# A 2-layer hybrid decoder step: the sample state products as stacked fp32r products, and the feed-forward norm factor applied behind the products

## The chip, the cores and the metric

The program runs on one core of a Trainium2 chip. The metric is the device time of one launch in microseconds; before and after are each timed in several runs, and the median is compared. Engine names are those of the profile: PE (TensorE matmul), PEld (its weight loads), DVE (VectorE), ACT (ScalarE), POOL (GpSimd), SP (SyncE, which here only issues transfers).

## The reference

Two layers; each layer maps 256 prompt tokens and 32 sample tokens (8 sequences of 4) of width 1024, together T = 288 columns. A layer is feed-forward (FFN) 1, token mixing, FFN 2:

```
def rmsnorm(x, g):
    y = xf * rsqrt(mean(xf * xf) + eps);  return y * g
def swiglu(x, w13, w2):
    a, b = split(x @ w13);  return (silu(a) * b) @ w2
x = x + 0.5 * swiglu(rmsnorm(x, f1n), f1w13, f1w2)
x = x + token_mixing(rmsnorm(x, mn), ...)
x = x + 0.5 * swiglu(rmsnorm(x, f2n), f2w13, f2w2)
```

Part of token mixing is the SSD scan, a recurrence over 32 heads in 8 groups. For the sample tokens it updates a state per sequence and head, h = exp(sum dt*A) h + sum over tokens of (dt x decay) B^T. It is all fp32.

## The kernel before

Activations lie feature-major: a tile of 128 features by 288 columns. An fp32 weight product is made of three fp32r products, weights high half by activations high half, high by low, low by high (`product`, lines 1425 to 1427); the weight halves are made on the chip. Weights come in units of 128 x 2048 in two slots s = 0, 1. For each unit SP loads `raw[s]`, ACT copies it to `w_hi[s]` (`high_unit`, line 676, after PE is done with the slot's previous unit), then DVE (`low_unit`, line 931) or POOL (line 1346) subtracts to `w_lo[s]`, and PE runs 48 matmuls of 288 columns on it. In the FFNs the low halves are DVE's; in the mixing stage they are mostly POOL's. Semaphores order everything; each engine runs its own list in order.

FFN: `norm` on PE sums squares of x (8 tiles, fp32 products with `ones`, line 1510) after ACT has squared them (line 683); ACT takes the root (687), DVE the reciprocal (962) and eight multiplications x * gain * rinv (966), ACT copies to `u_hi` (693), DVE subtracts to `u_lo` (958). Only then does the first weight product start. All of this waits for `add_to_x` (993), which adds the last stage's products to x. `swiglu` then runs 11 pairs of units of w13 (per pair: gate unit in banks 0, 1, up unit in banks 2, 3; silu on ACT, line 701, from PSUM; product and split on DVE, 981, 941, 943), and then the units of w2.

At the top of each layer SP loads ten small tables (`vec_a`, `vec_b`, `rows3`: taps, biases and gains) ahead of the first weights, and PE turns them behind the norm's sums.

SSD: per group g of 8, PE turns tiles of x and B to token-major (1526), DVE scales them (`a_tri` 1215, `xdt` 1230, `xdte` 1240, `xdte_s` 1243), builds `b_diag` (1250), a block-diagonal [32, 8 x 128] matrix with B of each sequence, ACT takes exponentials. After the prompt's products comes, for each of the two tiles t of the group: turn the old state (`state_turn`), two fp32 products `b_diag` by `xdte_s` of 512 columns each (line 1843), then products with the turned state (1850), a copy by ACT (`tok_rows`, 882) and `rows_turn`; DVE updates the state (1279), and the group's last DVE operation, line 1292, lets PE start the next group. Between these, PE runs three half units `side(3g..3g+2)` of unrelated weight products as filler, whose evacuations (846, 849) and weight copies (676) share ACT with the SSD, and whose low halves POOL makes. At the stage's start ACT copies `conv_out` (831) and POOL sends it out by DMA (1391, 1393).

Of the kernel before, what the change touches and what calls it, by code (L numbers as in the profile page):

```python
# [23 lines left out]
P = 128  # L24
# [83 lines left out]

def side_unit(n):

    return (True, n // 3) if n % 3 == 1 else (False, n - (n + 1) // 3)


def constants():
# [10 lines left out]
    small = np.zeros((TS, 2 * TS + NB), f)  # L125
    small[:, :TS] = same & (j[:, None] <= j[None])
    small[:, TS:TS + NB] = j[:, None] // NT == np.arange(NB)[None]
    small[:, TS + NB:] = same & (j[:, None] > j[None])
# [55 lines left out]
def trunk(nc, x_prompt, x_sample, cache_kv_w128, cache_kv_w512, cache_kv_w2048, state_conv, state_ssm,  # L184
# [9 lines left out]

    SKEWED = P * (W_LINE + 1)
# [5 lines left out]
    def place(name, shape, dt=F32, at=None):  # L201
# [3 lines left out]
        if at is None:  # L205
# [23 lines left out]
    small = place("small", [TS, 2 * TS + NB])  # L229
    ident, ones, tri, sgt = (square[:, n, :] for n in range(4))  # L230
    tri_sel_s, sel_s, tri_s, sgt_s = (small[:, 0:TS + NB], small[:, TS:TS + NB], small[:, 0:TS],
                                      small[:, TS + NB:])
# [11 lines left out]
    dt_fm = place("dt_fm", [HEADS, T])  # L244
# [52 lines left out]
    hidden = r("hidden", [P, 2, T])  # L297
    y_out = place("y_out", [P, 2, D], at=F_AT)
# [31 lines left out]
    xdt_s = r("xdt_s", [TS, 256])  # L330
    xdte_s = r("xdte_s", [TS, 256])
    b_tm_s = r("b_tm_s", [TS, NS])
    b_diag = r("b_diag", [TS, NB, NS])
# [7 lines left out]
    y_sq = place("y_sq", [P, KI, T], at=R2 + 4 * 1440)  # L341
# [3 lines left out]
    assert print_free > 24000  # L345
# [3 lines left out]
    with ExitStack() as ctx:  # L349
# [9 lines left out]
        x_first = sem("x_first", 0)  # L359
# [15 lines left out]
        vec_in = sem("vec_in", 16 * 10)  # L375
        vec_turned = sem("vec_turned", 1, 1)
        vec_ready = sem("vec_ready", 1)
        rows_used = sem("rows_used", 1, 1)

        squared = sem("squared", 3 * 4)  # L380
        sum_ready = sem("sum_ready", 3)
        rms_ready = sem("rms_ready", 3)
        normed_part = sem("normed_part", 3 * 4)
# [51 lines left out]

        ssd_turned = sem("ssd_turned", G)
# [60 lines left out]
        def _(sp):  # L497
# [25 lines left out]
            sp.dma_start(small[:], c_small).then_inc(const_in.sem, 16)  # L523

            with sp.Fori(0, DEPTH) as l:

                sp.wait_ge(vec_turned.sem, l + 1)
                settle(sp)
                sp.dma_start(vec_a[:], conv_w[bass.ds(l, 1)].rearrange("a i (t c) -> (a i t) c", c=P))\
                    .then_inc(vec_in.sem, 16)  # L530
                for row, v in ((V_CONVB, conv_b), (V_F1, ffn1_norm), (V_MIX, mix_norm), (V_F2, ffn2_norm),
                               (V_SSD, ssd_norm)):
                    n = v.shape[1] // P
                    sp.dma_start(vec_b[row:row + n, :], v[bass.ds(l, 1)].rearrange("a (t c) -> (a t) c", c=P))\
                        .then_inc(vec_in.sem, 16)
                sp.dma_start(vec_b[V_FIN:V_FIN + KD, :], final_norm.rearrange("(t c) -> t c", c=P))\
                    .then_inc(vec_in.sem, 16)
                sp.wait_ge(rows_used.sem, l + 1)
                settle(sp)
                for n, v in enumerate((dt_bias, a_log, d_skip)):  # L540
                    sp.dma_start(rows3[:, n, :], v[bass.ds(l, 1)].broadcast_to((P, HEADS)))\
                        .then_inc(vec_in.sem, 16)
# [106 lines left out]
                with sp.Fori(0, PAIRS_WO) as i:  # L649
                    rows(m + (M_WO + i), w_o, l, i * 512)  # L650
                with sp.Fori(0, PAIRS_W13) as i:
                    panel(m + (M_W13B + i), ffn2_w13, l, i * 256, FF + i * 256)
# [14 lines left out]
        def _(act):  # L667
# [9 lines left out]

            def norm(l, n, ready, m):
# [11 lines left out]
                for part in range(4):  # L690
                    tiles = slice(2 * part, 2 * part + 2)
                    wait(act, normed_part, l, 4 * n - 3 + part)
                    act.activation(u_hi[:, tiles], full[:, tiles], ACT.Copy).then_inc(u_hi_ready.sem, 1)

            def swiglu(l, m0, e0, n0):
                def body(i):
                    high_unit(0, l * PAIRS + (m0 + 1 + i))

                    act.wait_ge(unit_done[0].sem, l * PAIRS + (m0 + 2 + i))
                    act.wait_ge(evac[1].sem, l * EVACS + (e0 + 1 + i))  # L700
                    act.activation(silu_a[:], ps[:, 0:2, 0:T], ACT.Silu).then_inc(evac[0].sem, 1)
                    high_unit(1, l * PAIRS + (m0 + 1 + i))
                with act.Fori(0, PAIRS_W13) as i:
                    body(i)
# [12 lines left out]
            with act.Fori(0, DEPTH) as l:  # L717
                m = l * PAIRS

                act.wait_ge(x_first.sem, 4)  # L720
                norm(l, 1, R_W2B - ROWS, m)
                swiglu(l, M_W13A, E_W13A, 0)
# [5 lines left out]
                act.activation(dt_fm[:], ps[0:HEADS, 0, 0:T], ACT.Copy).then_inc(evac[0].sem, 1)  # L728
# [43 lines left out]
                act.activation(to_end[0:TS, 3, :], ps[0:TS, 4, 224:256], ACT.Exp).then_inc(to_end_ready.sem, 1)  # L772
# [80 lines left out]
                wait(act, kv_out, l, 16 * 6)  # L853
                for g in range(G):
                    wait(act, ssd_turned, l, g + 1)
                    for c in range(2):
                        act.activation(b_tm[:, c, :], ps[:, 7, c * P:(c + 1) * P], ACT.Copy)
                    act.activation(b_tm_s[:], ps[0:TS, 7, 256:384], ACT.Copy).then_inc(b_ready.sem, 1)
# [53 lines left out]
                norm(l, 3, R_WO, m + M_W13B)  # L912
                swiglu(l, M_W13B, E_W13B, PAIRS_W13)
# [13 lines left out]
        def _(dve):  # L927
# [24 lines left out]

            def norm(l, n, gain):
# [20 lines left out]
            def swiglu(l, m0, e0, n0):  # L974
                with dve.Fori(0, PAIRS_W13) as i:
                    low(l * PAIRS + (m0 + 1 + i))
                    dve.drain()

                    dve.wait_ge(evac[0].sem, l * EVACS + (e0 + 2 + i))
                    dve.wait_ge(unit_done[1].sem, l * PAIRS + (m0 + 2 + i))  # L980
# [967 lines left out]
```

## Time and profile before

| | us |
|---|---|
| median of 3 runs | 2414.03 (2411.07 to 2414.3) |
| profiled execution, its own time | 2411.02 |
| span in the profile, first to last instruction | 2408.9 |
| PE busy, share of the span | 90% |
| DVE, ACT, POOL busy | 53%, 41%, 17% |

The span and the profiled execution's own time differ by 2.1 us, which lies around the instructions. A busy PE is not PE at its peak: a row's duration of a matmul is its latency, and the spacing of many matmuls is read from a window and a count.

### The profile page before, as it was taken

To read this page: it belongs to the slowest core of one execution; us is meant where nothing else is said; L and a number is where in the kernel's file an instruction comes from. 1 tells how busy PE (TensorE), PEld (TensorE's weight loads), DVE (VectorE), ACT (ScalarE), POOL (GpSimd) and SP (SyncE) were. 2 spreads that over 40 slices of the span, in tenths; PEclk is the share of its full clock that TensorE was granted. 3 is DMA by queue.
4 is the path that set the end of the run, shared out by engine and by line. 5 is a ranking of instruction groups with operands and counts; after the bars stand their busy time and mean duration, and the time that the engine had idled before them with its cause. 6 is when DMAs were issued, how large, how long until landed. Compare 5 with 4: busy or idle time off the path is not lost.

```text
span 2408.9 us, 38626 instructions
## 1 busy us (share of the span) xinstructions
PE 2166.7 (90%) x15100; PEld 2000.4 (83%) x15100; DVE 1283.7 (53%) x1936; ACT 996.8 (41%) x1153; POOL 414.4 (17%) x162
## 2 busy tenths in 40 slices
PE   7999899987889888899899989999798888969996
PEld 5999889975767688899889989899676667969996
DVE  3553455765666472554355443575666665444543
ACT  3552434344344432554355443343433434235532
POOL 2000002202332455000000000121122224630000
PEclk9999999888999999999999999897998899989998
DMA  6444544423333333354434436442333332434541
GB/s 205 162 160 149 172 145 135 136 71 106 114 115 118 99 123 123 122 167 164 142 124 161 156 128 196 143 131 88 92 93 112 118 116 92 156 105 141 172 157 55
DMA packets 258232, 317.06 MB, mean 132 GB/s; under 512 B 9070, under 2 KB 232846, under 8 KB 258010
## 3 DMA queue, kind: packets, MB, share of 16 engines
q1 hardware_dynamic: 249656, 287.92, 37.0%
q0 software_dynamic: 7776, 26.73, 3.7%
q8 instruction: 77, 1.26, 0.2%
q10 hardware_dynamic: 680, 0.80, 0.1%
q14 instruction: 43, 0.35, 0.0%
HBM read 291.44 MB, written 26.33 MB: 132 GB/s over the span
## 4 chain that ended last, share of the span: by engine, by line
PE 69%; DVE 11%; ACT 5%; PEld 5%; issue 4%; POOL 3%; DVEq 1%; DMA 1%; SPq 1%; PEldq 0%; ACTq 0%; POOLq 0%
PE ps L1425 18%; PE ps L1427 17%; PE ps L1426 17%; PE ps L1526 5%; ACT w_hi L676 3%; POOL w_lo L1346 3%; PE ps L1843 2%; DVE flat L1292 2%; DVE w_lo L931 2%; PEld ps L1701 1%; PE ps L1510 1%; PEld ps L1425 1%; PE ps L1791 1%; PEld ps L1426 1%; PEld ps L1427 1%
## 5 line engine op out<-in xcount | busy, mean ns | idle before, releaser
L1425 PE MATMUL ps<-u_hi,w_hi 128*128 128x288 f32 x2736 | 851.8, 311 | 51.3 <-DVE u_lo L958 39.8
L1426 PE MATMUL ps<-u_lo,w_hi 128*128 128x288 f32 x2736 | 833.0, 304 | 0.0
L1427 PE MATMUL ps<-u_hi,w_lo 128*128 128x288 f32 x2736 | 830.2, 303 | 0.0
L676 ACT ACTIVATE w_hi<-w_raw 128x2048 fp32r<-128x2048 f32 x249 | 476.3, 1913 | 657.1 <-PE ps L1427 628.8
L931 DVE TENSOR_TENSOR w_lo<-w_raw,w_hi 128x2048 fp32r<-128x2048 f32 x172 | 394.3, 2292 | 549.1 <-ACT w_hi L676 549.1
L1425 PEld LDWEIGHTS ps<-u_hi,w_hi 128*128 128x128 f32 x2736 | 539.1, 197 | 62.0 <-issue 56.9
L1426 PEld LDWEIGHTS ps<-u_lo,w_hi 128*128 128x128 f32 x2736 | 540.4, 198 | 0.7
L1427 PEld LDWEIGHTS ps<-u_hi,w_lo 128*128 128x128 f32 x2736 | 539.9, 197 | 0.0
L1346 POOL TENSOR_TENSOR w_lo<-w_raw,w_hi 128x2048 fp32r<-128x2048 f32 x77 | 355.6, 4618 | 612.9 <-ACT w_hi L676 612.7
L1425 PE MATMUL ps<-h_hi,w_hi 128*128 (+1 forms) x704 | 209.2, 297 | 14.6 <-DVE w_lo L931 14.6
L1427 PE MATMUL ps<-h_hi,w_lo 128*128 (+1 forms) x704 | 207.9, 295 | 0.0
L1426 PE MATMUL ps<-h_lo,w_hi 128*128 (+1 forms) x704 | 207.8, 295 | 0.0
L1383 POOL DMA_DIRECT2D out_dram<-kv_p x6 | 4.1, 678 | 852.3 <-DVE kv_s L1093 852.1
L1425 PEld LDWEIGHTS ps<-h_hi,w_hi 128*128 128x128 f32 x704 | 132.8, 189 | 17.4 <-DVE w_lo L931 11.5
L1426 PEld LDWEIGHTS ps<-h_lo,w_hi 128*128 128x128 f32 x704 | 132.9, 189 | 0.0
L1427 PEld LDWEIGHTS ps<-h_hi,w_lo 128*128 128x128 f32 x704 | 132.7, 188 | 0.0
L1114 DVE SCALAR_TENSOR_TENSOR acc<-flat,conv_wt,acc 128x312 f32<-128x312 f32 x192 | 104.5, 586 | 7.3
L1279 DVE SCALAR_TENSOR_TENSOR h<-h,e_s,ps 128x128 f32<-128x128 f32 x256 | 68.9, 341 | 54.7 <-PE ps L1843 54.7
L1425 PE MATMUL ps<-y_hi,w_hi 128*128 128x288 f32 (+1 forms) x256 | 78.8, 308 | 9.4 <-POOL w_lo L1346 9.4
L676 ACT ACT_TABLE_LOAD x45 | 57.7, 1283 | 69.5 <-DMA w_raw<-in_ffn_w_dram 69.4
L1427 PE MATMUL ps<-y_hi,w_lo 128*128 128x288 f32 (+1 forms) x256 | 77.2, 302 | 0.0
L1426 PE MATMUL ps<-y_lo,w_hi 128*128 128x288 f32 (+1 forms) x256 | 77.2, 301 | 0.0
(273 smaller groups left out, 2706.4 us busy)
## 6 DMA issues: line engine op xcount, KB each, us to landing
w_raw<-in_ffn_w_dram SPq DMA_DIRECT2D x128, 1024.0 KB, 5.0
w_raw<-in_w_in_dram SPq DMA_DIRECT2D x82, 1024.0 KB, 5.3
h<-in_state_ssm_dram SPq DMA_DIRECT2D x32, 512.0 KB, 4.1
out_dram<-h POOLq DMA_DIRECT2D x32, 512.0 KB, 3.9
w_raw<-in_w_ssd_out_dram SPq DMA_DIRECT2D x16, 1024.0 KB, 4.8
kv_in<-in_cache_kv_w_dram SPq DMA_DIRECT2D x32, 256.0 KB, 4.2
w_raw<-in_w_o_dram SPq DMA_DIRECT2D x8, 1024.0 KB, 4.8
w_raw<-in_ffn_w_dram SPq DMA_DIRECT2D x8, 512.0 KB, 3.3
```

The costliest lines, as they stand in the source:

```text
L676: act.activation(w_hi[s][:], raw[s][:], ACT.Copy).then_inc(hi_ready[s].sem, 1)
L931: dve.tensor_tensor(w_lo[s][:], raw[s][:], w_hi[s][:].bitcast(F32), ALU.subtract)\
L1114: last = dve.scalar_tensor_tensor(out=dst, in0=src, scalar=tap, in1=dst, op0=ALU.mult, op1=ALU.add)
L1279: dve.scalar_tensor_tensor(out=h0[tile % 3][:, b, :], in0=h0[tile % 3][:, b, :], scalar=e_s[:, t, TS + b:TS + b + 1], in1=ps[:, 6 + b // 4 ...
L1292: last = dve.scalar_tensor_tensor(out=flat[:, tile, TP:T], in0=flat[:, tile, TP:T], scalar=skip[:, tile:tile + 1], in1=off_s[:, t, :], op0 ...
L1346: pool.tensor_tensor(w_lo[s][:], raw[s][:], w_hi[s][:].bitcast(F32), ALU.subtract)\
L1425: pe.matmul(out, wh, hi, start=first, stop=False)
L1426: pe.matmul(out, wh, lo, start=False, stop=False)
L1427: return pe.matmul(out, wl, hi, start=False, stop=last)
L1510: last = pe.matmul(ps[:, 0, 0:T], ones, full[:, k, :], start=(k == 0), stop=(k == KD - 1))
L1526: return pe.transpose(out, src, square[0:p, 0, 0:p])
L1843: last = pe.matmul(ps[:, 6 + n, :], xdte_s[:, t * P:(t + 1) * P], b_diag[:, 4 * n:4 * n + 4, :].rearrange("p b n -> p (b n)"), start=True, ...
```

## The change

1. FFN norm (FFN 1 and FFN 2 of both layers; the mixing norm stays as it was). `u = x * gain` is split at once, without the factor rinv: ACT writes `u_hi` with eight scaled copies, DVE writes `u_lo` with eight scalar_tensor_tensor, and PE starts `first_unit`, which goes over k outside and the two banks inside. The squares of x are taken by ACT in one activation behind that, DVE adds the eight tiles in three operations, PE sums over partitions with one fp32 product after the first pair of units. DVE's `gate` multiplies the gate product by rinv from PSUM to `a_in`, ACT's silu reads `a_in` from SBUF, and DVE's `up` multiplies silu by rinv and then by the up product. The first pair of units uses banks 0 to 3, the second 4 to 7, and the loop follows from the third. In the loop DVE makes the low half of slot 1 behind `up` instead of before it. The low half of slot 1 of FFN 2's first pair goes from POOL to DVE.
2. The small tables are gathered by 13 POOL transfers at the very start into `vec_tables` in DRAM; the first layer's are loaded by SP before the loop, each next layer's by two transfers ahead of FFN 2's weights, and PE turns them in FFN 2. SP keeps three small loads at the top of the layer.
3. SSD, sample part: `xdte_s` and `b_tm_s` are made on 96 partitions, three copies of the 32 tokens (POOL's `stack_sample` copies the columns three times, and a transpose puts them on partitions). `x_stack` holds high, high, low and `b_stack` high, low, high in fp32r, so that one fp32r product over 96 partitions gives the three partial products. `b_diag` is built from `b_stack`. The tiles `x_stack`, `b_stack`, `b_diag` and others take the memory of `conv_out`, so DVE and ACT wait for `conv_done_out` before group 0.

```diff
-            def panel_unit(s, m, norm=None):
+            def first_unit(l, n, m):
+                pe.wait_ge(lo_ready[0].sem, m + 2)
+                for k in range(KD):
+                    if k % 2 == 0:
+                        u_part(l, n, k // 2)
+                    for o in range(2):
+                        last = product(ps[:, o, 0:T], 0, k * 256 + o * P, u_hi[:, k, :], u_lo[:, k, :], k == 0,
+                                       k == KD - 1)
...
+                first_unit(l, n, l * PAIRS + m0)
+                panel_unit(1, l * PAIRS + m0)
+                wait(pe, ffn_summed, l, n // 2 + 1)
+                pe.matmul(ps[:, 7, 0:T], ones, full[:, 0, :], start=True, stop=True).then_inc(sum_ready.sem, 1)
+                panel_unit(0, l * PAIRS + (m0 + 1), 4)
+                panel_unit(1, l * PAIRS + (m0 + 1), 4, last_bank)
+                panels(l, m0, e0, PAIRS_W13, 2)
...
+            def ffn_norm(l, n, gain, m):
+                for part in range(4):
+                    wait(dve, u_hi_ready, l, 4 * n - 3 + part)
+                    for k in (2 * part, 2 * part + 1):
+                        last = dve.scalar_tensor_tensor(out=u_lo[:, k, :], in0=x[:, k, :], scalar=vecs[:, gain + k:gain + k + 1],
+                                                        in1=u_hi[:, k, :].bitcast(F32), op0=ALU.mult, op1=ALU.subtract)
+                low_unit(1, m)
+                wait(dve, ffn_squared, l, n // 2 + 1)
...
+                def gate(i, bank):
+                    dve.wait_ge(unit_done[0].sem, l * PAIRS + (m0 + 2 + i))
+                    dve.tensor_tensor(a_in[:], ps[:, bank:bank + 2, 0:T], scale, ALU.mult).then_inc(evac[0].sem, 1)
+                def up(i, bank, tiles):
+                    dve.wait_ge(silu_ready.sem, l * silu_ready.per + (n0 + 1 + i))
+                    dve.tensor_tensor(hidden[:], silu_a[:], scale, ALU.mult)
+                    dve.tensor_tensor(hidden[:], hidden[:], ps[:, bank + 2:bank + 4, 0:T], ALU.mult)
+                    split(h_hi[:, tiles, :], h_lo[:, tiles, :], hidden[:]).then_inc(h_ready.sem, 1)
+                with dve.Fori(2, PAIRS_W13) as i:
+                    gate(i, 0)
+                    low_unit(0, l * PAIRS + (m0 + 1 + i))
+                    up(i, 0, bass.ds(i * 2, 2))
+                    low_unit(1, l * PAIRS + (m0 + 1 + i))
...
+                wait(dve, conv_done_out, l, 32)
...
+                    dve.drain()
+                    dve.tensor_copy(x_stack[:], xdte_s[:])
                     wait(dve, b_ready, l, g + 1)
+                    dve.tensor_tensor(b_stack[B_LO], b_tm_s[B_LO], b_stack[B_LO].bitcast(F32), ALU.subtract)
+                    dve.drain()
+                    dve.tensor_tensor(x_stack[X_LO], xdte_s[X_LO], x_stack[X_LO].bitcast(F32), ALU.subtract)
...
-                            last = pe.matmul(ps[:, 6 + n, :], xdte_s[:, t * P:(t + 1) * P],
+                            last = pe.matmul(ps[:, 6 + n, :], x_stack[:, t * P:(t + 1) * P],
```

## Rows read from the trace of the kernel before

**Rows 1.** The page's chain that ended last, by engine.
```profile
PE 69%; DVE 11%; ACT 5%; PEld 5%; issue 4%; POOL 3%; DVEq 1%; DMA 1%; SPq 1%; PEldq 0%; ACTq 0%; POOLq 0%
```

**Rows 2.** Waits of PE: line, waited for, us in total, times, longest.
```profile
PE ps L1425 <- DVE u_lo L958: 39.8, 6, 9.3
PE ps L1526 <- DVE flat L1292: 30.9, 8, 4.4
...
PE ps L1802 <- DVE xdte_s L1243: 13.9, 4, 3.5
```

**Rows 3.** Windows: stretch, length, busy PE, PEld, DVE, ACT, POOL; clock, DMA, GB/s.
```profile
60.00:170.00 110.00, 110.00 (x827) 110.00 (x827) 55.43 (x42) 62.35 (x45) 0.00 (x0) 1.00 0.50 166
977.70:986.70 9.00, 8.98 (x49) 8.93 (x50) 3.69 (x7) 2.66 (x3) 0.00 (x0) 0.71 0.25 87
```

**Rows 4.** Timeline at FFN 2 of layer 0: start, us, engine and line.
```profile
962.72 2.75 DVE L993 SCALAR_TENSOR_TENSOR x<-ps,x 128x576 f32<-128x576 f32 x4 [22.47 <-PE ps L1427]
968.97 1.95 DVE L962 RECIPROCAL rinv<-rms 128x288 f32<-128x288 f32 x1 [3.50 <-ACT rms L687]
971.01 5.47 DVE L966 SCALAR_TENSOR_TENSOR full<-x,vecs,rinv 128x288 f32<-128x288 f32 x3
...
975.54 1.36 DVE L966 SCALAR_TENSOR_TENSOR full<-x,vecs,rinv 128x288 f32<-128x288 f32 x3
...
977.72 0.58 PE L1425 MATMUL ps<-u_hi,w_hi 128*128 128x288 f32 x1 [9.32 <-DVE u_lo L958]
```

**Rows 5.** Timeline from layer 0 to layer 1, FFN 1.
```profile
1184.12 0.34 SPq L529 DMA_DIRECT2D vec_a<-in_conv_w_dram  x1
...
1189.17 0.39 SPq L502 DMA_DIRECT2D w_raw<-in_ffn_w_dram  x1
...
1195.95 1.91 ACT L676 ACTIVATE w_hi<-w_raw 128x2048 fp32r<-128x2048 f32 x1 [6.18 <-DMA w_raw<-in_ffn_w_dram]
...
1201.62 2.77 PE L1510 MATMUL ps<-full,square 128*128 128x288 f32 x5 [6.04 <-ACT full L683]
...
1212.81 0.58 PE L1425 MATMUL ps<-u_hi,w_hi 128*128 128x288 f32 x1 [5.32 <-DVE u_lo L958]
```

**Rows 6.** Timeline at the start of the program.
```profile
27.00 0.54 DVE L1012 TENSOR_TENSOR lines<-ps,line_mask 4x384 f32<-4x384 f32 x1
...
37.56 0.58 PE L1425 MATMUL ps<-u_hi,w_hi 128*128 128x288 f32 x1 [5.32 <-DVE u_lo L958]
```

**Rows 7.** Groups over the span: count, busy us, mean ns, idle before.
```profile
L931 DVE TENSOR_TENSOR w_lo<-w_raw,w_hi 128x2048 fp32r<-128x2048 f32 x172 | 394.3, 2292 | 549.1 <-ACT w_hi L676 549.1
...
L701 ACT ACT_TABLE_LOAD x44 | 56.5, 1283 | 0.8
```

**Rows 8.** Timeline in an odd SSD group of layer 0 (g = 3).
```profile
665.97 1.21 DVE L1250 TENSOR_TENSOR b_diag<-b_tm_s,small 32x1024 f32<-32x1024 f32 x1
...
673.57 1.98 PE L1843 MATMUL ps<-b_diag,xdte_s 32*128 32x512 f32 x4
673.68 1.02 ACT L877 ACTIVATE h_t<-ps 128x1024 f32<-128x1024 f32 x1 [0.41 <-PE ps L1526]
```

**Rows 9.** Timeline at the end of an even SSD group (g = 2).
```profile
651.12 1.90 ACT L676 ACTIVATE w_hi<-w_raw 128x2048 fp32r<-128x2048 f32 x1
...
654.35 4.65 DVE L1292 SCALAR_TENSOR_TENSOR flat<-flat,skip,off_s 128x32 f32<-128x32 f32 x1
654.41 4.53 POOL L1346 TENSOR_TENSOR w_lo<-w_raw,w_hi 128x2048 fp32r<-128x2048 f32 x1
```

**Rows 10.** Start of the SSD stage of layer 0 (timeline).
```profile
558.03 1.65 DVE L1215 TENSOR_SCALAR a_tri<-square,da 128x128 f32<-128x128 f32 x8
...
564.18 0.51 POOL L1393 DMA_DIRECT2D out_dram<-conv_out  x1
...
566.28 2.07 PE L1791 MATMUL ps<-a_tri,square 128*128 128x512 f32 x4
```

**Rows 11.** The page's DMA issues: count, KB each, us to landing.
```profile
out_dram<-conv_out POOLq DMA_DIRECT2D x2, 384.0 KB, 5.1
```

More of the change, by code:

```diff
@@ L329, in trunk @@
     h_end = r("h_end", [P, 2, NS])
[L330 to L333, printed above, removed]
+    r = Plan(R1 + 20736 + 12288)
+    stack_in = [r(f"stack_in{n}", [P, 3, STACK, TS]) for n in range(2)]
     cbm_s = r("cbm_s", [TS, TS])
@@ L340, in trunk @@
     assert r.now <= R2, r.now - R2
-    y_sq = place("y_sq", [P, KI, T], at=R2 + 4 * 1440)
+    r = Plan(R1)
+    xdt_s = r("xdt_s", [TK, 256])
+    xdte_s = r("xdte_s", [TK, 256])
+    x_stack = r("x_stack", [TK, 256], F32R)
+    b_tm_s = r("b_tm_s", [TK, NS])
+    b_stack = r("b_stack", [TK, NS], F32R)
+    b_diag = r("b_diag", [TK, NB, NS], F32R)
+    assert r.now <= R1 + 16384
+    y_sq = place("y_sq", [P, KI, T], at=229344 - 4 * KI * T)
     y_rms = place("y_rms", [P, G, T], at=R2 + 4 * 4 * T)
@@ L676, in high_unit, with ffn_norm @@
                 act.activation(w_hi[s][:], raw[s][:], ACT.Copy).then_inc(hi_ready[s].sem, 1)
+            def ffn_norm(l, n, ready, gain, m):
+                wait(act, vec_ready, l, 0)
+                for o in range(4):
+                    wait(act, row_evac, l, ready + o + 1)
+                    for k in (2 * o, 2 * o + 1):
+                        last = act.activation(u_hi[:, k, :], x[:, k, :], ACT.Copy,
+                                              scale=vecs[:, gain + k:gain + k + 1])
+                    last.then_inc(u_hi_ready.sem, 1)
+                high_unit(1, m)
+                act.activation(full[:], x[:], ACT.Square).then_inc(ffn_squared.sem, 1)
+                act.activation(warm[:], eps[:], ACT.Sqrt)
             def norm(l, n, ready, m):
@@ L1028, in _ @@
                     low(m + (M_QKV + 1 + i))
-                wait(dve, vec_in, l, 160)
+                wait(dve, rows_in, l, 48)
                 wait(dve, dt_turned, l, 1)
@@ L1543, in _ @@
                 new = OLD + g * TS
-                pe.matmul(ps[:, 1, g * TS:(g + 1) * TS], lhs, hot[:, new:new + TS], start=True, stop=True)
-                last = pe.matmul(ps[0:HPG, (2, 3, 7)[g], 0:W_LINE], rel4[0:32, 4 * g:4 * g + 4], line_hot[:, g, :],
+                at = W_LINE + g * TS
+                pe.matmul(ps[:, 7, at:at + TS], lhs, hot[:, new:new + TS], start=True, stop=True)
+                last = pe.matmul(ps[0:HPG, 5 + g, (P, P, 0)[g]:(P, P, 0)[g] + W_LINE], rel4[0:32, 4 * g:4 * g + 4], line_hot[:, g, :],
                                  start=True, stop=True)
@@ L1815, in _ @@
                         at = 352 + (h // 2) * 64
-                        pe.matmul(ps[half, 3, at:at + TS], xdt_s[:, h * HD:(h + 1) * HD], dec_s[:, h, :], start=True,
+                        pe.matmul(ps[half, 3, at:at + TS], xdt_s[0:TS, h * HD:(h + 1) * HD], dec_s[:, h, :], start=True,
                                   stop=True)
```

279 lines of the change are left out of this document (180 added, 99 removed).

## The prediction

> **What bounds the kernel.** I read the chain that ended last first: 69% of it is PE, 11% DVE [rows 1]. So PE sets the time, and where DVE or ACT stands on the chain PE is waiting for it. The windows say how full PE is: in the w13 loop of FFN 1, 110 us hold 827 matmuls without a gap at full clock (2.4 GHz) [rows 3], which is 0.133 us for 288 columns, 0.46 ns a column, and 6.4 us for a unit of 48. Nothing is to be gained there; it can only be lost. The waits of PE then say where it stands still [rows 2]: 39.8 us for `u_lo` behind the norms (six norms, of which the change touches four), 30.9 us at the starts of SSD groups for line 1292, 13.9 us for `xdte_s`. The timelines give the price of each.
>
> **FFN norms.** *FFN 2 of layer 0.* The last product ends at 962.7; the first of w13 comes at 977.72, 15.0 us later, of which PE spends 4 on column sums [rows 4]. The middle is slow: three multiplications of line 966 take 5.47 us, three later ones 1.36 [rows 4]; POOL's low half runs then, and [rows 9] show the same thing, a DVE operation with two SBUF inputs standing still as long as POOL's subtraction runs. The change takes root, reciprocal, sums and this collision out of the way. What stays: `add_to_x`, 2.75 us to 965.47; ACT's scaled copies run beside it; then `u_lo`, 0.45 us each [rows 4], two for the first part, so PE starts near 966.5. That is 11.2 us earlier. A part gives PE 12 matmuls (1.6 us, more at half clock) and DVE needs 0.9 for the next, so PE does not starve. The first unit takes 9.0 us before, at a mean granted clock of 0.71 [rows 3]; behind a stop of 3.8 instead of 15 us I take 0.7 off that, between 0 and 2.6.
>
> Against it: (a) the one fp32 sum product. Two fp32 products of 512 columns take 1.98 us [rows 8], so 288 columns take 0.56. (b) A new chain behind it: root about 0.5 (an estimate, below the 1.02 of a 1024-column ACT copy [rows 8]), reciprocal 1.95 [rows 4], low half of slot 1 2.3, gate 0.7, table load 1.28 and silu 0.7, three operations of `up` 2.1, gate of the second pair 0.7, low half of slot 0 2.3 ([rows 7] for low half and table load; 576 columns cost 0.69 us each in the four of 2.75 us of [rows 4]). That is 12.5 us, and with some ten drains and hops between engines, 0.1 to 0.2 us each by estimate, 14.3. PE has two units, 12.8, to cover it: 1.5 us of waiting, bounds 0 and 3. (c) At the start of w2 the low half of slot 1 now stands behind three operations, 2.3 to 2.5 us, instead of behind only ACT's copy of 1.9 [rows 5]: 0.6 us. (d) FFN 2 also turns the tables, two fp32 turns of 128 columns, four passes each by the fp32 price above: 0.45. So FFN 2 gains 11.2 + 0.7 - 0.56 - 1.5 - 0.6 - 0.45 = 8.8 us, twice: 17.6.
>
> In the loop DVE works 55.43 us in 8.6 pairs [rows 3], 6.4 us a pair of 12.8; two operations more of 0.7 to 0.8 make it 8.0. The low half of slot 1 ends about 11.1 us after gate's unit, needed at 12.8; the one of slot 0 at 4.3, needed at 6.4. I cost the loop at nothing; PE's own 12.8 us hide it. If that cover failed by 1 us a pair, 44 pairs would cost 44 us.
>
> *FFN 1 of layer 1.* PE ended at 1195.6 (1201.62 less 6.04) but DVE reaches `add_to_x` only at 1200.1, since its list holds the first low half of the new layer, whose weights SP issued only at 1189.17, behind ten small transfers from 1184.12 on [rows 5]. Three stay; the weights go out near 1186, land 3.3 us sooner, and `add_to_x` starts near 1196.4. First product at 1200.2 instead of 1212.81, 12.6 us; with + 0.7 - 0.56 - 1.5 - 0.6 it is 10.6 us.
>
> *FFN 1 of layer 0.* DVE finishes the bias lines at 27.5 [rows 6] and then makes `u_lo`. PE has 0.5 us of table turns more ahead of them. First product near 27.5 + 0.5 + 0.9 + 0.1 = 29.0 instead of 37.56, 8.5; with + 0.2 - 0.56 - 1.5 - 0.6 it is 6.0. POOL's 13 transfers lie under the loading of x; at 0.51 us of issue as in [rows 10], or at twice that, they end before PE has turned x.
>
> Sum of the FFNs: 17.6 + 10.6 + 6.0 = 34 us, bounds 22 and 46.
>
> **SSD.** *Removed.* An fp32 pair of 512-column products takes 1.98 us to the end of the last record [rows 8], four passes of 0.47, about 1.9. In fp32r the two take 2 x 512 x 0.46 ns = 0.47, one pass as the weight products' [rows 3], so 1.4 less, in 32 tiles: 45 us at most. Should fp32r of 512 columns over 96 partitions pay the four passes again, nothing is gained; the weight products are the nearest row and I go by them. Not all of it lies on the path. For t = 0 the next product also needs ACT's copy of the turned state, 673.68 + 1.02 = 674.70 [rows 8], and PE was free at about 675.5: only 0.7 counts. For t = 1 in odd groups all 1.4 counts. For t = 1 in even groups the path goes elsewhere: ACT evacuates the filler and makes `w_hi` from 651.12 to 653.02, only then copies `tok_rows`; POOL's low half starts at 654.41 and DVE's line 1292, 0.06 us ahead of it on paper, stands until it ends, 4.65 us [rows 9]. PE's products earlier by 1.4 let POOL start its own transfer earlier, but not ahead of ACT's copy: POOL's low half can move by 1.2 to 1.4 us at most, and line 1292 still falls into it. Even groups gain 0.7 + 1.2 = 1.9, odd ones 2.1.
>
> *Added on DVE:* a copy, two subtractions and drains, about 1.1 us ahead of `b_diag` (1.21 us and no longer on 96 partitions [rows 8]). In most groups the exponentials or the filler product cover all but 0.15; in one group a layer where `b_diag` itself meets POOL it costs 1.1. *Added on POOL:* two small copies per group, some 0.8 us. The rows show only POOL's long two-input subtraction stopping DVE; whether short one-input copies do, they don't show. Bounds 0 and 0.8 us a group; I take 0.4 in odd groups, where DVE has the least room. The Trainium skill (GPSIMD Engine Reference, Specifications) says that the SBUF interface is shared with VectorE instructions that have two SBUF inputs or run in a 2-port mode; by it the stack copies would stop DVE in every group, and the sum would be 13 us worse if each lay on the path, and `x_stack`'s copy could be stopped as well. The trace agrees for two inputs [rows 9].
>
> Per layer: even 4 x 1.9 = 7.6; odd 4 x (2.1 - 0.15 - 0.4) = 6.3; less 1.1: 12.8.
>
> *The new wait.* Group 0 waits on DVE and ACT for `conv_done_out`. POOL issues the second transfer at 564.18 [rows 10] and it takes 5.1 us [rows 11], to 569.3. Before, `a_tri` and what follows ran from 558.03, under ACT's copies. Now its 1.65 us and the small ones behind it, some 2.7 in all, start at 569.4 and end at 572.1, when PE wanted them at 566.28 [rows 10]: 5.8 us, and a PE at rest so long restarts at half clock as in [rows 3], 1.4 more. Behind the waiting DVE stand `xdt` and all of group 0. Cost 7.2 us a layer, bounds 5 and 9.
>
> So SSD gains 12.8 - 7.2 = 5.6 a layer, 11 us in both, bounds -6 and 26.
>
> **Sum.** 34 + 11 = 45 us. On the profiled execution, 2411.0 - 45 = 2366; on the median of the runs, 2414.0 - 45 = 2369.
>
> **Rivals.**
> 1. *The state products pay in full.* The meetings of DVE and POOL hang on tenths of a microsecond (0.06 us in [rows 9]). If line 1292 or `xdte_s` escapes POOL's low half in half of the groups, up to 20 of the 44.8 us [rows 2] come back: 2414 - 45 - 22 = 2347. For: the timing shifts by over 1 us. Against: POOL follows ACT and PE, so that it shifts along. 15%.
> 2. *SSD gives nothing or loses.* More groups meet POOL (the stack copies, 1.1 us more of two-input work on DVE ahead of PE's next need), each meeting 3.5 us plus restart: with 5 more of 16 groups hit, -20 us: 2389. For: DVE's list is longer exactly where PE waits. Against: the added work lies behind `xdt_ready`. 17%.
> 3. *Slower.* The w13 loop loses its cover: low half of slot 1, ready 1.7 us ahead of need by my count, gives out if DVE's drains or the landing of the next weights are later than I think. From 1.05 us a pair on (46 us over 44 pairs) the kernel is slower; at 1.5 us it takes 2414 - 45 + 66 = 2435. For: the change puts two more operations on DVE and a chain DVE, ACT, DVE into each pair. Against: 12.8 us a pair against 8.0 of work [rows 3]. 5%.
> 4. *The norm's part does not do what it says*, since the chain behind the sum product stops PE by over 6 us in each FFN: 2414 - 45 + 20 = 2389. 5%.
>
> **Chances.** Forecast 58%, rivals 15, 17, 5, 5. What a measurement of this kernel can tell from no change is about 0.2%, 5 us. Faster by more 0.92 (the forecast, rivals 1, 2 and 4, less a tail), within 0.02, slower 0.06. The range takes in rivals 1, 2 and 4 with the bounds of the SSD terms: 2336 to 2397; the forecast's own is 2355 to 2383.
>
> **What would show it.** The first w13 product 3.8 us behind the last product in FFN 2 and some 4.6 in FFN 1 of layer 1; a wait of 1 to 2 us ahead of the third pair; the w13 loop still 0.133 us a matmul; line 1843 with two records of about a quarter of the time; `a_tri` of group 0 near 6 us later with a PE stop of that size; line 1292 still near 4.6 us in even groups. I am wrong if the loop has gaps, if line 1292 is short, or if group 0 doesn't wait.

## The result, and the profile after

The changed kernel takes 2357.28 us (median of 4 runs, 2356.91 to 2359.15) against 2414.16 for the kernel before on the same chip, a ratio of 0.9765 with a 95% interval of 0.9748 to 0.9782: 57 us faster. Forecast were 2369.0 and a range of 2336 to 2397. The profiled execution took 2357.22 us with a span of 2355.5, so 53.4 us of span are to be placed. (The profiled execution before, 2411.02 us, is the fastest of its four; 3.5 us of the 57 are not in the two profiles.)

The page's chain that ended last, by engine, hardly moved [rows 1]: the kernel is still bound by PE.

```profile
PE 68%; DVE 11%; ACT 5%; PEld 5%; issue 4%; POOL 3%; DMA 2%; DVEq 1%; PEldq 0%; SPq 0%; ACTq 0%; POOLq 0%
```

The waits of PE after (waited for: us in total, times, longest), to be laid beside [rows 2]:

```profile
PE ps L1548 <- DVE w_lo L979: 22.4, 15, 4.7
PE ps L1957 <- DVE xdte_s L1333: 20.9, 6, 3.5
PE ps L1680 <- DVE flat L1387: 20.5, 8, 3.0
...
PE ps L1548 <- DVE u_lo L1006: 15.2, 4, 4.8
PE ps L1680 <- ACT h_mid L930: 14.3, 8, 1.8
...
PE ps L1946 <- DVE a_exp_s L1312: 13.6, 8, 5.8
PE ps L1680 <- DMA small<-in_c_small_dram: 13.3, 1, 13.3
```

`u_lo` fell from 39.8 us to 15.2 (four FFN norms) and 10.3 (the two mixing norms, which were not touched). `flat` fell by a third and the copy of the rows (h_mid, L930) took its place. `a_exp_s` with its 5.8 is the new wait of group 0. `w_lo` with a longest of 4.7 is new, and nobody had forecast it.

I cut both spans at the same points of PE's timeline (starts of the same products). The stretches, in us:

```
stretch                                        before   after   gain   forecast
start to first product                          37.56   32.09    5.5      8.5
rest of FFN 1, layer 0                         218.59  226.46   -7.9     -2.5
turn to FFN 2, FFN 2, FFN 1 of layer 1         498.07  474.38   23.7     19.4
turn to FFN 2, FFN 2, end, layer 1             291.20  279.27   11.9      8.8
SSD with its norm, layer 0 / layer 1    307.26/308.28  301.18/298.80   15.6   11
attention, layer 0 / layer 1            139.28/145.24  139.31/142.36    2.9    0
all others                                                       1.7      0
sum                                                             53.4     45
```

**FFN 2 of layer 0**, to be laid beside [rows 4]:

```profile
960.21 2.75 DVE L1084 SCALAR_TENSOR_TENSOR x<-ps,x 128x576 f32<-128x576 f32 x4 [23.09 <-PE ps L1550]
963.87 0.40 PE L1548 MATMUL ps<-u_hi,w_hi 128*128 128x288 f32 x1 [3.70 <-DVE u_lo L1006]
978.26 0.65 PE L1654 MATMUL ps<-full,square 128*128 128x288 f32 x2
979.48 1.95 DVE L1061 RECIPROCAL rinv<-rms 128x288 f32<-128x288 f32 x1
981.26 1.28 ACT L736 ACT_TABLE_LOAD   x1
988.78 2.28 DVE L979 TENSOR_TENSOR w_lo<-w_raw,w_hi 128x2048 fp32r<-128x2048 f32 x1
```

The first product comes 3.70 us behind the last one, not 15.0. Root, reciprocal and table load now stand beside PE's products. The last row is the low half for the third pair; it ends at 991.06, and PE comes to it at 991.75 without a gap.

**From layer 0 to layer 1**, beside [rows 5]:

```profile
1172.31 20.56 SPq L524 DMA_DIRECT2D w_raw<-in_ffn_w_dram  x4
...
1182.88 2.75 DVE L1084 SCALAR_TENSOR_TENSOR x<-ps,x 128x576 f32<-128x576 f32 x4
1186.57 0.61 PE L1548 MATMUL ps<-u_hi,w_hi 128*128 128x288 f32 x1 [4.77 <-DVE u_lo L1006]
```

The first weights of layer 1 go out at 1172.31. The forecast's "near 1186", less the 13.8 us by which all of it now comes sooner, is 1172.2. The first product follows at 1186.57, 4.77 us behind the last one.

**The start**, beside [rows 6]; this is where the forecast went wrong:

```profile
13.34 0.69 PE L1680 MATMUL ps<-square,x_in 128*128 128x128 f32 x2 [13.34 <-DMA small<-in_c_small_dram]
32.09 0.61 PE L1548 MATMUL ps<-u_hi,w_hi 128*128 128x288 f32 x1 [3.05 <-DVE u_lo L1006]
34.07 1.10 POOL L1472 DMA_DIRECT2D bias_skewed<-bias_lines  x1 [1.94 <-DMA bias_lines<-lines]
37.09 0.37 SPq L524 DMA_DIRECT2D w_raw<-in_ffn_w_dram  x1
54.04 1.91 ACT L701 ACTIVATE w_hi<-w_raw 128x2048 fp32r<-128x2048 f32 x1 [6.27 <-DMA w_raw<-in_ffn_w_dram]
58.33 0.61 PE L1548 MATMUL ps<-u_hi,w_hi 128*128 128x288 f32 x1 [4.72 <-DVE w_lo L979]
```

PE begins 3.3 us later than before (10.02), since the constants land later. Then the weights that SP issued at 37.09 are not there before 54, 17 us in place of a median of 5.0 on the page, and PE stands 4.72 us ahead of the fourth unit, the second of the second pair.

**SSD, the end of an even group** (g = 2), beside [rows 9]:

```profile
657.21 0.89 POOL L1532 DMA_DIRECT2D out_dram<-h  x1 [4.60 <-DVEq L1378]
658.06 0.36 ACT L930 ACTIVATE h_mid<-ps 128x256 f32<-128x256 f32 x1
658.24 4.53 POOL L1441 TENSOR_TENSOR w_lo<-w_raw,w_hi 128x2048 fp32r<-128x2048 f32 x1
658.48 0.44 PE L1680 MATMUL ps<-square,h_mid 128*128 128x128 f32 x2 [1.78 <-ACT h_mid L930]
659.48 3.33 DVE L1387 SCALAR_TENSOR_TENSOR flat<-flat,skip,off_s 128x32 f32<-128x32 f32 x1
662.87 0.55 PE L1680 MATMUL ps<-square,flat 128*128 128x128 f32 x3 [2.37 <-DVE flat L1387]
```

The meeting with POOL is still there, as forecast: a DVE operation of 0.25 us takes 3.33, to the end of POOL's subtraction. The wait for the rows, 1.78 us, is another: ACT copies them only at 658.06, behind the silu and its weight copy.

### The profile page after: what moved, and what is told of

It is laid out like the page before. It is cut to its first block, busy times and chain, and to the rows that moved or that the text cites. A ratio compares the mean times of both kernels' runs of the same rounds, so it can differ in the third digit from the quotient of the medians.

```text
span 2355.5 us, 38389 instructions
## 1 busy us (share of the span) xinstructions
PE 2102.4 (89%) x14982; PEld 1974.3 (84%) x14982; DVE 1342.7 (57%) x2072; ACT 888.8 (38%) x1075; POOL 422.6 (18%) x205
## 4 chain that ended last, share of the span: by engine, by line
PE 68%; DVE 11%; ACT 5%; PEld 5%; issue 4%; POOL 3%; DMA 2%; DVEq 1%; PEldq 0%; SPq 0%; ACTq 0%; POOLq 0%
PE ps L1548 19%; PE ps L1549 18%; PE ps L1550 18%; PE ps L1680 4%; POOL w_lo L1441 3%; ACT w_hi L701 3%; DVE w_lo L979 2%; DVE flat L1387 1%; PEld ps L1853 1%; PEld ps L1548 1%; PEld ps L1549 1%; PEld ps L1550 1%; PE ps L1946 1%; PE ps L1799 1%; DVE xdte_s L1333 1%
## 5 line engine op out<-in xcount | busy, mean ns | idle before, releaser
L1548 PE MATMUL ps<-u_hi,w_hi 128*128 128x288 f32 x2736 | 853.9, 312 | 42.5 <-DVE u_lo L1006 15.2
L1441 POOL TENSOR_TENSOR w_lo<-w_raw,w_hi 128x2048 fp32r<-128x2048 f32 x75 | 344.8, 4598 | 592.1 <-ACT w_hi L701 591.4
L1374 DVE SCALAR_TENSOR_TENSOR h<-h,e_s,ps 128x128 f32<-128x128 f32 x256 | 68.9, 340 | 19.7 <-PE ps L1998 19.6
L1200 DVE TENSOR_SCALAR acc<-flat,conv_wt,vecs 128x312 f32<-128x312 f32 x64 | 59.4, 968 | 27.1 <-ACT flat L788 27.1
```

Source lines behind the costliest of these rows:

```text
L1200: dve.tensor_scalar(dst, src, tap, vecs[:, V_CONVB + tile:V_CONVB + tile + 1], ALU.mult, ALU.add)
L1374: dve.scalar_tensor_tensor(out=h0[tile % 3][:, b, :], in0=h0[tile % 3][:, b, :], scalar=e_s[:, t, TS + b:TS + b + 1], in1=ps[:, 6 + b // 4 ...
L1441: pool.tensor_tensor(w_lo[s][:], raw[s][:], w_hi[s][:].bitcast(F32), ALU.subtract)\
L1548: pe.matmul(out, wh, hi, start=first, stop=False)
```

## The experiments

Each was timed in 5 runs (ffn_only in 4) beside the kernel before on its chip; the changed kernel's ratio of 0.9765 is what to lay them beside.

**One part alone.** stack_only is the kernel before with the SSD part, ffn_only with the FFN part.

> The kernel before with the stacked sample state alone (stack copies, one fp32r product for each half in place of two, wait for the conv transfer), its feed-forward halves as before. Theory: the two changes are independent, so this shows the state-space part's own gain as in the windows of the changed kernel's trace, 6.1 and 10.7 us: 2397 us. Rival: part of it came from weights and buffers that the new feed-forward hand-over frees earlier, and it gives 11 us or less: 2403 or more. The prediction's term was 11.

Measured: 2395.80 us, ratio 0.9927 [0.9914, 0.9941], 17.5 us faster, as the theory had it. SSD took 298.1 and 298.0 us. The changed kernel's 301.2 and 298.8 are high for this code: tables_late, bias_spread and recip_twice (below), which leave SSD as it is there, took 297.4 to 298.8 in all six passes. So a stretch of one profile is good to some 3 us here.

> The kernel before with the feed-forward part of the change alone: norm factors applied where the products leave, first unit walked by tiles of k, tables by way of DRAM; the state-space part as before. Theory: the stacked state alone gave a ratio of 0.9927 and both together 0.9765, the places differ, so this gives 0.984 to 0.985 of the kernel before, 36 to 39 us faster (the forecast's term was 34). Rival: the two parts share a gain (buffers and weights freed earlier at the turn of the stages), and this alone gives 30 us or less.

Measured: 2382.36 us, ratio 0.9865 [0.9843, 0.9886], 32.6 us faster, less than the theory's 36, with a forecast term of 34. The two ratios multiply to 0.9793, about 7 us short of both together, with intervals that leave it at the edge of chance. In its profile the SSD stretches, whose code is that of before, took 312.2 and 314.2 us instead of 307.3 and 308.3; the window of the first shows PE busy 272.4 us at a mean granted clock of 0.91, before 268.0 at 0.93. So much of these 10.8 us is clock, and not a shared gain. But this profile is of the slowest of the four runs (2387.17 us), and why this kernel got less of the clock is open.

**The new wait of group 0.**

```diff
-                wait(dve, conv_done_out, l, 32)        # ahead of group 0 (ACT likewise)
...
+                    if g == 0:
+                        wait(dve, conv_done_out, l, 32)
                     dve.tensor_tensor(xdt_s[:]...
```

> The changed kernel with the new wait for the conv state transfer moved, in group 0 of the state-space part of both layers, from ahead of everything on VectorE and ScalarE to ahead of the first write of the memory that the transfer reads (xdt_s on VectorE, b_tm_s on ScalarE). Nothing else changes. Theory: PE's waits of 5.42 and 5.83 us for a_exp_s at the start of group 0 come from this wait, because a_tri, a_exp and the rest were queued behind it; they go, and about 5 us a layer with them, 10 us in all: near 2347 us. A new wait of up to 2 us may appear at xdt_s. Rival: what PE waits for at that place is late anyway (the last convolved tile, the product for to_end), and only the name of the wait changes: within 1 us of 2357.

Measured: 2345.80 us, ratio 0.9721 [0.9708, 0.9735], which is 0.0044 or 10.6 us below the changed kernel's. The timelines of the changed kernel and of this one, layer 0:

```profile
570.85 1.66 DVE L1305 TENSOR_SCALAR a_tri<-square,da 128x128 f32<-128x128 f32 x8 [10.97 <-DMA out_dram<-conv_out]
573.54 1.22 PE L1946 MATMUL ps<-a_tri,square 128*128 128x512 f32 x1 [5.42 <-DVE a_exp_s L1312]
```
```profile
559.76 1.65 DVE L1305 TENSOR_SCALAR a_tri<-square,da 128x128 f32<-128x128 f32 x8
568.01 2.03 PE L1948 MATMUL ps<-a_tri,square 128*128 128x512 f32 x4
571.08 0.42 DVE L1326 TENSOR_TENSOR xdt_s<-ps,dt 96x256 f32<-96x256 f32 x1 [1.81 <-DMA out_dram<-conv_out]
573.15 0.70 PE L1959 MATMUL ps<-xdte,b_tm 128*128 128x256 f32 x2 [1.26 <-DVE xdte_s L1335]
```

DVE's `a_tri` comes 11 us earlier, and PE waits 1.26 us in place of 5.42. SSD fell to 294.4 and 291.9 us, 6.8 and 6.9 less than in the changed kernel's trace, 3 to 7 less than in the other traces with its SSD; by the times it is 5.3 a layer. With the rest of 1.26 that still stands, the cost was 5 to 8 us a layer; 7.2 was forecast.

**The start.** tables_late moves POOL's 13 table transfers behind the bias loads; bias_spread cuts the 2,304 KB transfer into 12, one a pair.

```diff
+            for h in range(NG * HPG + 1):
...
+                if h < NG * HPG:
+                    pool.wait_ge(unit_done[0].sem, h + 4)
+                    pool.dma_start(skewed[h:h + 1]...   # one head
```

> The changed kernel with POOL's 13 small table transfers moved from its start to behind the bias transfers (about 60 us in), so that nothing of the first 15 us but the 51 KB small table differs in its DMAs from the kernel before. Theory: the 13 transfers delay the constants, so PE's first work comes at 10.0 us again in place of 13.3, the first product near 29 in place of 32.1; but slot 1's weights for the second pair are late whatever the start does, so little of the 3.3 us reaches the end: 0.5 to 3.3 us faster. Rival: the 51 KB small table (9 KB before) delays them: the first work stays at 13.3 and the time at 2357.

> The changed kernel with the one 2,304 KB transfer that writes the skewed bias cut into 12 of 192 KB, one a head, each behind the first unit of one more pair of the first feed-forward half, and each followed by its head's load; nothing else. Theory: that transfer (issued at 34.07, 18.1 us to landing) holds back the weights issued at 36.9 and 44.9 and so makes PE's 4.72 us wait before 58.33 and the products at the low clock behind it; spread, the wait goes and the mixing norm starts 4 to 7 us earlier: 2350 to 2353 us. Rival: the weights are late because their slot comes free late: the wait stays within 1 us of 4.7 and the time at 2357; or the pieces hold up later weights and give the gain back.

Measured: tables_late 2354.11 us, 0.9751 [0.9738, 0.9765]; bias_spread 2351.57 us, 0.9739 [0.9719, 0.976]. By times alone both lie within or at the edge of the changed kernel's interval; the traces show the rest. In tables_late the first work comes at 10.81 and the first product at 29.56 (the forecast had 29.0), and PE then waits 5.31 us for the same weights, so that 2.7 us arrive at the mixing norm. In bias_spread the wait before the fourth unit is gone and the rest of FFN 1 takes 220.3 us in place of 226.5:

```profile
41.22 1.92 ACT L701 ACTIVATE w_hi<-w_raw 128x2048 fp32r<-128x2048 f32 x1 [8.73 <-PE ps L1552]
...
48.50 1.91 ACT L701 ACTIVATE w_hi<-w_raw 128x2048 fp32r<-128x2048 f32 x1
```

The weights issued at 36.99 are there by 48.50. The collision with the bias transfer cost 6.1 us in this stretch; of it, the standing still is 4.72 and the rest the clock behind it.

**How much of the state products is on the path.**

```diff
-                        for n in range(2):
+                        for n in (0, 1, 0, 1):
```

> The changed kernel with each pair of stacked state products issued twice into the same banks (32 pairs more of some 0.55 us at the full clock, 17.6 us of PE work), the output unchanged. Theory: behind the first tile's pair PE waits 0.65 us for ScalarE's copy h_t in all 16 groups, and behind the even groups' second pair 1.78 us for ScalarE's copy of the rows, so an added pair is hidden in 24 of 32 places and is paid in the odd groups' second tile: 8 x 0.55, 4 to 7 us slower with what VectorE's update of the state starts later: 2361 to 2364 us. Rival: every pair lies on the path (as the forecast of this change took it for the pairs removed, 1.98 to 0.7 each): 15 to 20 us slower, 2373 or more.

Measured: 2373.15 us, 0.984 [0.9825, 0.9854], 16 to 18 us slower: the rival's number. The trace does not place it there. The pair costs 0.43 to 0.5 us; two groups take 60.9 us instead of 60.4, and the SSD stretches took 305.2 and 300.3 us, 5.5 more in sum than in the changed kernel and 8 to 10 more than in the four other traces with its SSD code. That lies between the theory (4 to 7) and the rival (15 to 20), so how many of the 32 places pay is not settled. Another 6 us of the profile's 16 lie in attention (142.4 and 145.2 us), whose code is the same. That it came in all five runs (2369 to 2377) I cannot explain; it is told below what that stretch does in all kernels.

**Whether POOL's stack copies hold DVE back.**

> The changed kernel with POOL's two stack copies of each group issued twice, with a drain between (16 x 0.7 us more of POOL, more where they meet VectorE). Theory: POOL's single-input copies cost VectorE nothing (in the trace they are the ones stretched, 0.42 to 1.20 us, where both are at work) and POOL has slack: within 1.5 us of 2357. Rival: each copy holds VectorE back, in a stretch where VectorE is what PE waits for: 16 x 0.7 or more, 2368 us.

Measured: 2354.89 us, 0.9765 [0.9751, 0.9778]: no difference. The forecast's 0.4 us in each odd group was not there. Where a stack copy meets DVE it is mostly the copy that stretches: in the changed kernel 0.35 us alone and up to 1.21 beside DVE, in this one up to 2.02.

**POOL's low halves.** The waits for `flat` and `xdte_s` stand beside a low half of POOL; that for the rows stands behind ACT's list, which the first of these kernels changes as well.

```diff
+                    if g:
+                        side_low(3 * g // 2 + 2 if g % 2 else (3 * g - 2) // 2 + 2)   # on DVE
                     wait(dve, y_product, l, g + 1)
...
                         dve.drain().then_inc(h_new_ready.sem, 1)
+                        if t and g % 2 == 0:
+                            side_low(3 * g // 2 + 2)
```

> The changed kernel with the low halves of the side weights in groups 0 to 7 of the state-space part made on VectorE (2.29 us) in place of POOL (4.5 us), put where VectorE waits for PE: ahead of its wait for the y products (one in each group but the first) and, in even groups, ahead of its wait for the second tile's rows; in even groups ScalarE also makes the high half and copies the rows before it takes the silu. Theory: VectorE makes no two-input operation while POOL makes a low half (the operation of line 1387 took 3.3 us and xdte_s 4.7 us in place of 0.25 and 0.41 in these places), and that is what PE's waits for flat (20.5 us), for xdte_s (20.9 us) and half of those for the rows (14.3 us) are; they go but for a third, with the low clock behind some of them: 25 to 40 us faster, 2317 to 2332 us. Rival: VectorE has no room (it is busy with the state updates), the 2.29 us each are then paid 23 times, and PE waits for off_t and h instead: within 10 us of 2357, or slower.

> The changed kernel with ScalarE's order alone changed in even groups (high half of the side weights, then the copy of the rows, then the silu with its table load), the low halves left on POOL. Theory: the rows come 1.4 us earlier, but POOL's low half then starts behind the high half 1.7 us earlier too, and VectorE's three operations that follow the rows fall inside it as before, so the wait ends when POOL ends: 1.4 to 2 us a group pair, 8 x that at most, 0 to 15 us faster (2342 to 2357). Rival: the order of ScalarE, and not who makes the low halves, is what made the kernel with the low halves on VectorE 64 us faster: 2310 us or less.

> The kernel before, not the changed one, with the side weights' low halves on VectorE and ScalarE's order as in the changed kernel with them. Theory: the loss by POOL's low halves is the same in both kernels (waits for flat 30.9 us, xdte_s 13.9, dec_s 5.9 before), so this gains about as much, 50 to 65 us, 2350 to 2362, and the whole change on top of it is worth 57 us as it was. Rival: the stacked products' gain was partly cover for these stalls: with the stalls gone the state products of before (1.98 us each in 32 places) lie fully on the path, the change is then worth 75 us or more, and this kernel stays above 2365.

Measured: dve_lows 2291.16 us, 0.95 [0.9487, 0.9514], 64 us below the changed kernel, more than the theory's 40. rows_first 2369.33 us, 0.9811 [0.9789, 0.9832], 11 us slower than the changed kernel, a miss. before_dve_lows 2350.11 us, 0.9732 [0.9712, 0.9752], 65 us below the kernel before. In dve_lows, at the end of an even group (g = 2):

```profile
649.48 0.37 ACT L933 ACTIVATE h_mid<-ps 128x256 f32<-128x256 f32 x1
650.11 2.29 DVE L990 TENSOR_TENSOR w_lo<-w_raw,w_hi 128x2048 fp32r<-128x2048 f32 x1
652.84 0.25 DVE L1405 SCALAR_TENSOR_TENSOR flat<-flat,skip,off_s 128x32 f32<-128x32 f32 x1
653.15 0.55 PE L1697 MATMUL ps<-square,flat 128*128 128x128 f32 x3 [1.17 <-DVE flat L1405]
```

The operation that took 3.33 us takes 0.25. Two groups take 50.3 us (602.81 to 653.15) in place of 60.4 (602.49 to 662.87), and all of SSD 263.8 and 267.9 us in place of 301.2 and 298.8. The windows of 60 us, the changed kernel and dve_lows, show where the theory was too low: PE has fewer gaps and also runs at the full clock all the time between them. Over both SSD stretches PE's idle time falls by 41 us (102.4 to 61.4) and its busy time for the same products by 27 (497.5 to 470.2, at a mean granted clock of 0.97 and 0.95 in place of 0.91 and 0.92).

```profile
603.00:663.00 60.00, 50.77 (x390) 42.51 (x389) 43.97 (x120) 25.83 (x43) 20.54 (x13) 0.92 0.42 126
```
```profile
603.00:663.00 60.00, 55.68 (x444) 45.89 (x444) 50.43 (x154) 29.61 (x53) 7.39 (x12) 1.00 0.51 157
```

rows_first says why order alone did nothing at its place (two groups 60.5 us, SSD 300.2 and 300.4):

```profile
659.22 0.89 POOL L1543 DMA_DIRECT2D out_dram<-h  x1 [4.60 <-DVEq L1389]
659.51 5.19 DVE L1398 SCALAR_TENSOR_TENSOR flat<-flat,skip,off_s 128x32 f32<-128x32 f32 x1
660.13 4.51 POOL L1452 TENSOR_TENSOR w_lo<-w_raw,w_hi 128x2048 fp32r<-128x2048 f32 x1
```

POOL's low half was not waiting for ACT: it stands in POOL's list behind the transfer of `h`, which waits for DVE. So it stayed; the rows came earlier, and DVE stood 5.19 us in place of 3.33. The 11 us are not in this stretch, and their cause is open; all five runs had a mean granted clock of 0.930 to 0.933, against 0.937 to 0.939 of the changed kernel. before_dve_lows settles the last question: the loss is as large without the stacked products, and the change on top of it is worth a ratio of 0.95 to 0.9732, which is 0.9762, as it was. What no run separates is ACT's order once the low halves are DVE's: PE's waits for the rows, 14.3 us in the changed kernel, are gone in dve_lows as well, and the new order may have its part in that. The Trainium skill (Perfetto Trace Analysis, Optimizing Scalar/DVE Operations) says that GPSIMD and DVE share an SBUF read port, so that offloading between them might not help. The runs agree: taking these subtractions off POOL, with ACT's order, gave 64 us.

**The chain behind the sum of squares.**

```diff
                 dve.reciprocal(rinv[:], rms[:])
                 dve.drain()
+                dve.reciprocal(rinv[:], rms[:])
+                dve.drain()
```

> The changed kernel with VectorE's 1.95 us reciprocal of each feed-forward norm made twice (four times in all), the output unchanged. It measures what cover the chain behind the sum of squares has left. Theory: in layer 0's second half slot 0 of the third pair is ready at 991.06 and PE comes to it at 991.9, 0.8 us of cover; 1.95 more costs 1.1 us in three of the four feed-forward halves and nothing in the first (its weights are late): 3 to 6 us slower, 2360 to 2363. Rival 1, as the forecast's working had it (chain 14.3 against a cover of 12.8): no cover is left and all four pay in full, 8 us or more. Rival 2: there is more cover than it seems, and it stays within 1 us.

Measured: 2364.49 us, 0.9799 [0.9781, 0.9817], 7 to 8 us slower. In the trace, ahead of the second unit of the second pair (979.40) and of the third pair (986.57) of FFN 2 in layer 0, where the changed kernel has no gap:

```profile
979.40 0.37 PE L1550 MATMUL ps<-u_hi,w_hi 128*128 128x288 f32 x1 [0.46 <-DVE w_lo L979]
...
986.57 0.40 PE L1550 MATMUL ps<-u_hi,w_hi 128*128 128x288 f32 x1 [0.54 <-DVE w_lo L979]
```

The same in layer 1's two halves (0.60 and 0.61, 0.46 and 0.54), and none more in the first one, where the wait for the weights stays (4.64): 3.2 us in all, where the theory said. So the 1.95 us used up a cover of 0.8 to 1.0, and not of nothing, as rival 1 had it, though the time alone is at the rival's 8. The stretches with these three halves are 4.9 us longer. The profile is of the fastest of the five runs, 3.5 us above the changed kernel's, so it cannot place the rest of the 7 or 8.

**All that helped, together:** low halves on DVE, the late wait, the tables late, the bias spread, and the small table moved back in its queue.

> The low halves on VectorE, the late wait for the conv transfer, POOL's table transfers late and the skewed bias spread, all in one, with the 51 KB small table also moved behind the first vectors in its queue (so that the transposes of x wait for the 256 KB constants and x alone). Theory: places differ, so the gains add: the gain of the low halves alone, plus 11.5 for the wait, plus 8 to 9 for the start, each as measured: about 20 us below the kernel with the low halves alone. Rival: the group-0 wait and the low halves overlap (both end at VectorE), or the start is bound by the order of the first weights: 10 us or less below it.

Measured: 2268.05 us (2264.26 to 2273.55), 0.9409 [0.9395, 0.9424], 23 us below dve_lows. SSD took 256.8 and 257.8 us, the first product came at 29.38 and the rest of FFN 1 took 220.2. This version beats both kernels: by the ratios 86 us below the changed one, 143 below the one before.

## Why the prediction was right, and where only in sum

45 us were forecast and 57 measured. Of the 12 between them, 4.6 lie in SSD, 4.6 in stretches that the change does not touch, 3.5 outside the two profiles, and the FFNs gave 0.8 less.

**FFN, 34 us forecast, 33.2 in the profile, 32.6 for the part alone.** The sum is right because two errors cancel. *The turns* were right: 15.0 to 3.7 us of gap (forecast 3.8), and 12.5 in FFN 1 of layer 1 (from the last product of w2 to the first of w13 17.23 to 4.77 us; forecast 12.6). *The costs behind* were too high, by 2 to 3 us in each of three halves. (b), 1.5 us of waiting, is nothing: ACT takes silu's table load at 981.26, while DVE makes a low half, so its 1.28 us are not in the chain, which takes 12.2 us from the end of the sum product (978.91 to 991.06) and not 14.3. recip_twice shows that some 0.8 to 1 us of cover was left. (c), 0.6, was 0.23 (1.22 to 1.45 us at the start of w2). (a) and (d) take 0.6 us together, from 978.26 to the next product at 978.88, forecast 1.0. *The start* failed: forecast +6.0, measured -2.4. The step was that POOL's 13 transfers "lie under the loading of x", and the term had no place at all for the next weights. tables_late shows that the 13 transfers hold the constants back by 2.5 us and that the forecast's 29.0 for the first product stands without them; bias_spread shows that the new order, with the first products sooner, puts the second pair's weights beside the 2,304 KB bias transfer, for 6.1 us. The row for it was there before: that transfer went out at 30.56, and the weights behind it at 43.80, when most of it had landed. In the changed kernel they follow it by 3 us.

**SSD, 11 us forecast, 15.6 in the profile, 17.5 for the part alone.** Against the traces of the four other kernels with this SSD code it is 18 to 20. The new wait was sized about rightly (7.2; PE's wait itself 5.42 and 5.83, forecast 5.8; conv_late). fp32r of 512 columns over 96 partitions runs in one pass, as assumed: the second of a pair starts 0.23 to 0.32 us behind the first (512 columns at 0.46 ns are 0.24), and the pair takes 0.62 to 0.71 us to the end of the second record instead of 1.98. What was undersized is what the products give: 25.6 us (2 x 12.8) by forecast without the wait (its odd groups add up to 6.2 and not 6.3, so 12.7 a layer); conv_late, without it, has SSD 29.3 us shorter than before (615.5 to 586.3), with a rest of the wait still in it. VectorE's state update waited for the products 54.7 us in all before and 19.6 after. Of the terms taken off, 0.4 an odd group for POOL's copies was nothing (copies_twice); the 0.15 for DVE's list and the 1.1 where `b_diag` meets POOL were not measured alone. Line 1387 stayed in POOL's shadow, as said; PE waits 2.4 to 3.0 us there, and 1.78 for the rows instead.

**Rivals.** 1 (half of the meetings escape) did not come true: none went away. But dve_lows shows that its price was far too low. It put 44.8 us of waits in play. With the low halves on DVE and ACT's new order 64 us come back; in the SSD stretches PE stands 41 us less, near the rival's sum, and the 27 us on top are the same products at a higher clock, which the rival did not price. 2 (more meetings) did not: six groups are held at their head, at `xdte_s` now, before four there and two at `dec_s`. 3 did not: the loop holds its pace (797 products in 106 us, 0.133 each). 4 did not.

**What of the 53.4 us is not the change.** 2.9 us lie in attention of layer 1, which the change doesn't touch, and 1.7 in the other stretches outside the FFNs and SSD.

## What to carry to other kernels

Before a long subtraction goes to POOL because POOL is idle, see what DVE does in those 4.5 us. In these traces an operation with both inputs in SBUF stood until the subtraction ended (0.25 us became 3.33, 0.41 became 4.74), and so did some copies and scalings from SBUF to SBUF; one with an input from PSUM did not (`off_s`, 0.19 us beside it as elsewhere). A DVE pass of half the length, put where DVE waits anyway, with ACT's order, gave more here than the whole change. When a stage is made to start sooner, list the large transfers that were issued in the time it gives up, and ask which loads now go out beside them. And a wait for memory to come free belongs right ahead of the first write into it, not at the head of the stage.

## What the runs showed of the hardware

**The same work takes 139.3, 142.3 or 145.2 us.** The stretch of attention from the first turned cache tile to the first scores of the prompt took one of these three in 26 of the 28 passes of the fourteen traces, in both layers and whatever was changed (twice 143.9). In the changed kernel layer 0 has the short one and layer 1 the middle one. Up to 441.28 and 1588.32 us, the same point of the work, the two passes keep within 0.2 us of each other, and the 9 us before that have a granted clock of 0.81 in both. In the next 9 us PE is busy throughout in both, but there are 69 products in the one and 59 in the other, at a granted clock of 1.00 and 0.81. What decides it no run shows.

```profile
441.28:450.28 9.00, 9.00 (x69) 8.84 (x69) 8.61 (x16) 3.53 (x7) 0.00 (x0) 1.00 0.71 226
```
```profile
1588.32:1597.32 9.00, 9.00 (x59) 8.88 (x57) 8.62 (x16) 3.53 (x7) 0.00 (x0) 0.81 0.73 232
```

The two passes together took 278.6 us in bias_spread and 290.5 in before_dve_lows, so profiles can differ by 12 us by this alone, and single profiles should be compared stretch by stretch.

**A single-input DVE operation stands too.** In double_state the cast of `x_stack`, 0.29 us alone, took 4.50 beside POOL's subtraction, which itself took 5.53 in place of 4.53; two operations of DVE (0.41 and 0.75 us) still passed at its start:

```profile
636.79 5.53 POOL L1441 TENSOR_TENSOR w_lo<-w_raw,w_hi 128x2048 fp32r<-128x2048 f32 x1 [4.80 <-ACT w_hi L701]
...
637.98 4.50 DVE L1340 CAST x_stack<-xdte_s 96x256 fp32r<-96x256 f32 x1
```

The kernel before shows it too: scaling by a tap from SBUF to SBUF (line 1111) took up to 4.14 us in place of 0.44 beside POOL, in 10 of 64 places. The Trainium skill (GPSIMD Engine Reference, Specifications) names two-input and 2-port operations as those that contend with GPSIMD. The two-input kind is seen throughout; whether the cast runs in a 2-port mode no run shows, though a cast of 1152 columns took 0.76 us where a two-input subtraction of them took 1.36. Which side gave way differed: beside POOL's subtraction it was mostly DVE, beside POOL's short one-input copies mostly the copy.
